# Attention stage of a hybrid encoder step: VectorE takes the low parts of step s-1 before the bias and maximum of step s+1, instead of after them

## The reference, cut to what matters

```python
def _fox_block(q, cq, qpos, k, v, ck_t, kpos):
    s = jnp.einsum('bthd,bshd->bhts', q, k) * (HEAD_DIM ** -0.5)
    bias = jnp.transpose(cq, (0, 2, 1))[..., :, None] - ck_t[:, :, None, :]
    mask = kpos[None, :] <= qpos[:, None]
    s = jnp.where(mask, s + bias, NEG_INF)
    pr = jax.nn.softmax(s, axis=-1)
    return jnp.einsum('bhts,bshd->bthd', pr.astype(v.dtype), v)
```

## Time and profile before

| | us |
|---|---|
| median of 3 runs (2385.41 to 2386.32) | 2385.94 |
| the profiled execution | 2386.21 |
| its span, first to last instruction | 2384.5 |
| TensorE busy | 2204.8 (92%) |
| VectorE busy | 1615.1 (68%) |
| ScalarE busy | 905.3 (38%) |
| GpSimd busy | 324.4 (14%) |
| attention stage, its eight heads | about 1203 to 1409 on the span's clock |

### The profile page before, as it was taken

The page is one execution under the profiler, slowest core; times in us unless marked ns, Lnnn a source line. Parts: engine busy times, 40 slices in busy tenths (PEclk is TensorE's granted clock), DMA queues, the critical chain, the costliest instruction groups (busy, mean ns, idle before and its releaser), DMA issues. The chain is left out here.

```text
span 2384.5 us, 44150 instructions
## 1 busy us (share of the span) xinstructions
PE 2204.8 (92%) x16355; PEld 2112.5 (89%) x16355; DVE 1615.1 (68%) x2941; ACT 905.3 (38%) x1843; POOL 324.4 (14%) x428
## 2 busy tenths in 40 slices
PE   3999999999899999999889978978989999999995
PEld 3999999999899999999878867978989987889995
DVE  6778766767786888876446646667657666667663
ACT  6542333333533333334366736234343331113112
POOL 0011000000111212111153410001111211111110
PEclk7999999999999999999989989989999999999997
DMA  8484444444757788786377655454556665346332
GB/s 245 145 260 111 141 131 131 149 122 143 263 187 201 225 227 230 221 231 176 112 237 226 204 176 185 131 200 148 190 207 234 217 217 164 110 123 207 103 97 98
DMA packets 362384, 424.80 MB, mean 178 GB/s; under 512 B 76064, under 2 KB 294792, under 8 KB 354336
## 3 DMA queue, kind: packets, MB, share of 16 engines
q1 hardware_dynamic: 306128, 266.62, 37.8%
q0 software_dynamic: 29504, 110.42, 13.5%
q10 hardware_dynamic: 26576, 45.40, 5.9%
HBM read 270.01 MB, written 143.68 MB: 173 GB/s over the span
## 5 line engine op out<-in xcount | busy, mean ns | idle before, releaser
L761 PE MATMUL acc<-t_act,w_hi 128*128 128x264 f32 x5376 | 888.6, 287 | 12.9 <-DVE zb L1323 5.2
L761 PEld LDWEIGHTS acc<-t_act,w_hi 128*128 128x128 f32 x5376 | 749.3, 189 | 19.5 <-issue 18.1
L761 PE MATMUL acc<-t_act,w_lo 128*128 128x264 f32 x2688 | 549.0, 286 | 0.0
L761 PEld LDWEIGHTS acc<-t_act,w_lo 128*128 128x128 f32 x2688 | 418.2, 189 | 0.0
L2764 PE MATMUL m_acc<-m_t_act,m_hi 128*128 128x264 f32 x1792 | 295.7, 288 | 19.4 <-ACT m_acc L2807 9.8
L1316 DVE TENSOR_TENSOR w_lo<-w_raw_f,w_hi 128x512 fp32r<-128x512 f32 x288 | 197.8, 687 | 143.7 <-ACT w_hi L971 143.4
L971 ACT CAST w_hi<-w_raw_f 128x512 fp32r<-128x512 f32 x288 | 177.9, 618 | 265.5 <-PE acc L761 245.0
L2764 PEld LDWEIGHTS m_acc<-m_t_act,m_hi 128*128 128x128 f32 x1792 | 252.7, 191 | 20.0 <-issue 20.0
L3171 PE MATMUL post_acc<-h_hi,w_post_hi 128*128 128x272 f32 (+1 forms) x768 | 210.9, 329 | 7.5 <-PEq L2573 4.3
L3171 PE MATMUL post_acc<-h_hi,w_post_lo 128*128 128x272 f32 (+1 forms) x768 | 208.2, 325 | 0.0
L3171 PE MATMUL post_acc<-h_lo,w_post_hi 128*128 128x272 f32 (+1 forms) x768 | 207.9, 325 | 0.0
(11 more groups left out here) (435 smaller groups left out, 3631.1 us busy)
## 6 DMA issues: line engine op xcount, KB each, us to landing
w_raw_f<-in_w_in_dram SPq DMA_DIRECT2D x96, 512.0 KB, 4.0
w_raw<-in_w_pg_dram SPq DMA_DIRECT2D x64, 512.0 KB, 4.7
cT<-zb SPq DMA_DIRECT2D x24, 1056.0 KB, 4.6
zb<-cT POOLq DMA_DIRECT2D x96, 264.0 KB, 5.8
zT<-zb POOLq DMA_DIRECT2D x80, 264.0 KB, 3.6
m_raw<-in_w_out_dram SPq DMA_DIRECT2D x32, 512.0 KB, 5.8
eT<-e_out ACTq DMA_DIRECT2D x16, 528.0 KB, 3.0
cT<-m_zb SPq DMA_DIRECT2D x8, 1056.0 KB, 5.0
```

Source lines behind the costliest of these rows:

```text
L761: mm = pe.matmul(out[:, c, 0:QN], w[:, k, :], t_act[:, SIDE[r], x, k, c * QN:(c + 1) * QN], start=(opens and k == 0 and m == 0), stop=(k = ...
```

## The change

On VectorE, in each of the eight steps of a head, the block with `low_parts` now stands ahead of the block with `bias`. Nothing is added or removed, no wait changes its condition, and the order of the other four engines is the same row for row.

```diff
             def head(h, hb, i, first=False, last=False):
                 for s in range(8):
-                    if s < 7:
-                        bias(h, s + 1, hb, i)
-                    elif not last:
-                        bias(h + 1, 0, 1 - hb, i + hb)
                     if first and s == 1:
                         for n in range(4):
                             dve.wait_ge(G["sem"][f"z_put{n}"], put_count(2 * NP - 1))
                     if s > 0:
                         low_parts(h, s - 1)
                     elif not first:
                         low_parts(h - 1, 7)
+                    if s < 7:
+                        bias(h, s + 1, hb, i)
+                    elif not last:
+                        bias(h + 1, 0, 1 - hb, i + hb)
                     if s == 1 and not first:
                         gate_out(h - 1, 1, 1 - hb)
```

## The result

The changed kernel took **2434.72 us** (median of 4 runs, 2431.32 to 2435.59), the kernel before 2386.13 us in the same comparison (4 runs, 2385.41 to 2391.34). The ratio is 1.0201, with a 95% interval of 1.0185 to 1.0218: slower by some 48.6 us. The forecast was 2429 us, in a range of 2415 to 2444. The profiled execution of the changed kernel took 2435.59 us, the slowest of the four, with a span of 2433.9 us.

What follows compares the result with a forecast made beforehand. TensorE, 95% busy, was taken to pace the attention stage. To 2386.21 us came 6.1 + 7 × 4.34 = 36.5 us for the VectorE-ScalarE ring, giving 2422.7, plus 6.5 for four clock falls: 2429 us, range 2415 to 2444.

Steps and rivals of the forecast that it cites:

- The ring: Steps 3 to 6: exponential, copy, high parts, low parts, bias, next exponential run serially; 16.00 us against 11.66, 4.34 a head.
- the first head: No earlier `weigh` covers steps 0 to 2, so all steps run serially: 21.24 us against 15.12, 6.1 us more.
- Steps 0 to 2 at nothing: Delays of about half a microsecond in steps 0 to 2 fall in idle time under the previous head's `weigh`; no cost.
- The last head: It has no copies for a next head; given the same 4.34 us as the others.
- The clock: TensorE's new pauses, about 2 us before step 7, lower its clock; four falls of 1.63 us taken, 6.5 us.
- one row each way: A 2.90 us stretch at the stage's end preceded a clock fall; a 1.60 us TensorE pause left it at 1.00.
- the prediction's rival: By the skill's rule the clock falls once or twice in every head: 2436 to 2449 us; twice has chance 0.12.
- The clock holds: Rival: TensorE's pauses stay too small to lower the clock; about 2423 us, chance 0.20.
- Two falls in every head: Rival: clock falls ahead of step 7 and in steps 4 and 5; 26.1 us extra, 2449 us, chance 0.12.
- Hidden: Rival: TensorE's work in steps 3 to 6 outlasts the serial VectorE-ScalarE chain, so nothing moves; 2386 us, chance 0.05.
- faster: Rival: earlier low parts free the transposes' banks and remove TensorE's waits, 5.3 us; 2381 us, chance 0.03.

Runs made afterwards that it cites:

- the run with the filler: Seven matmuls of 512 columns added on TensorE ahead of step 7's transposes in each head, against the changed kernel; 2425.80 us.
- the run with the copies behind: ScalarE's copies for the next head put behind the high parts in steps 3 to 6, against the changed kernel; 2418.42 us.

## Why the prediction was right, and where it was off

**What bounds the kernel.** The reading that the bias before the change runs in idle time of VectorE, and that the low parts lose nothing to it, was right. The low parts did not come earlier relative to their high parts in steps 3 to 6: in all eight heads they begin 0.03 us behind the first group, before and after, as forecast.

**The ring.** This step was right, in mechanism and size: 16.05 us against 16.00, and a head without a fall grew by 4.35 against 4.34. Steps 3 to 6 alone bring the whole loss, one step alone or every second step bring little, and taking 1.6 us of work out of the ring takes 1.6 us from a head. The estimates for the first head held too (21.32 against 21.24, 6.2 us more against 6.1). That the first period grew by 7.1 us is these 6.2, the 0.55 by which the mark moved, and the 0.34 put down to the execution. The second to the seventh head grew by 4.34 to 4.61 us between the high parts of step 2 and the low parts of step 6.

**Steps 0 to 2 at nothing.** Right for the heads with cover (25.09 against 25.05 with the change made there alone). In the first head they were in the sum. There the run with steps 0 to 2 alone gives them 1.07 us and the run with steps 3 to 6 alone gives those 5.12 (10.92 before, 16.04), which together is the 6.2 measured.

**The last head.** The prediction gave it the 4.34 us of the others, for want of a row. From the high parts of step 2 to the low parts of step 6 it took 14.44 us (1431.16 to 1445.60) where it took 9.54 (1388.03 to 1397.57): 4.90. It has no copies for a next head, so TensorE's step was shorter, and the ring in it as well.

**The clock.** This is the term that was mis-sized. The price of a fall was right where TensorE is on the path (1.63 forecast, 1.36 to 1.61 measured behind six heads, 1.6 at the stage's end), the number was not: four were taken, 6.5 us in all, and six came in the heads, 8.9 us. The forecast stood on one row each way and chose the middle. The row against a fall was also read too short: the 1.60 us of the earlier trace rows are cut out of a longer pause, which the clock came through at 1.00:

```profile
1800.35 0.72 PE L2764 MATMUL m_acc<-m_t_act,m_hi 128*128 128x264 f32 x4 [2.61 <-DVE m_zb L2944]
```

From 2429.2 to the 2435.59 of the profiled execution the steps are: falls 2.4 us, the ring of the second to the last head 1.1 (half of it in the last), the first head 0.1, the longer stretch at the stage's end 0.8, and 2.0 ahead of the low parts of the first step and behind the stage. The Trainium skill, "TensorE: Matmul & The Clock Gate", section "A second HAM failure mode: psum-queue depth-cycling", says of another kernel that short idling of TensorE between groups of matmuls, as it cycles through PSUM banks, lets the clock swing, at a price between bursts. The trace agrees that the clock swings, with a fall behind six heads. That the 2436 us of the prediction's rival, with one fall in each of eight heads, is 1.3 us above the measured median is luck: it has 13.0 us for falls, where 9.7 came, and the difference is made up by the other steps above.

**The rivals.** "The clock holds" is out, with six falls. "Two falls in every head" is out: there was one in each from the second head on. But its second place exists, as the run with the filler shows, and its price there was 0.9 us, partly hidden as the prediction's argument against it said. "Hidden" and "faster" are out by 48 us and more.

**What stays open.** Why a pause brings a fall in one head and none in the next. In the changed kernel the first head kept the clock and all later ones lost it, after the same pause of 1.74 us, and the stretches of 3.00 us ahead of `weigh(1)` read almost alike (TensorE busy 1.10 us in the first head, 1.14 in the fourth); with steps 3 to 6 alone the first head fell as well. In the run with the copies behind, three of seven nearly equal pauses (1.22 to 1.26 us) were followed by a fall. And at the stage's end TensorE pauses for 1.01 us in the kernel before and in the run with steps 0 to 2 alone, with the same instructions from there on, and only the first fell. The stretch that answers to the second of the earlier trace rows, in the run with steps 0 to 2 alone:

```profile
1399.16:1402.56 3.40, 3.40 (x16) 2.76 (x16) 1.01 (x3) 0.26 (x1) 0.00 (x0) 1.00 0.40 160
```

No run here settles what decides. That is why the count of falls could be bounded but not told.

## What to carry to other kernels

Before moving work ahead on an engine, ask whether the work it passes ran in a wait: work that fills a hole costs nothing, and the same work behind what ended the hole costs its full length. When two in-order engines hand to each other, write down one turn of the ring with every instruction that stands between, whatever it is for; the sum gave this case's ring to 0.05 us (16.00 against 16.05). And a pause that is new on TensorE can have two prices, the pause and the clock behind it. Look for the nearest pause on record for the likely number of falls, and keep none and one a turn as the bounds: here pauses of 1.74 us a head brought six and seven falls in seven heads, pauses of 1.2 us three, and pauses of 0.5 us none.

## What the runs showed of the hardware

- A pause of 1.74 us on TensorE, once in a head of 31 us, came with a fall to 0.50 for 3.4 us behind it in six of seven heads, and in seven of seven with steps 3 to 6 alone. A pause of 1.01 us at the stage's end came with one in two of six traces. A pause of 2.61 us in a later stage of the kernel before left the clock at 1.00.
- A fall of that length costs 1.4 to 1.6 us behind such a pause, and 0.9 us in steps 4 and 5, where TensorE had slack. Filling the pause with seven matmuls of 0.27 us each brought `weigh(1)` back to 0.39 us a matmul, and some falls came at another place where TensorE waits.
- The cause that the table of waits gives as issue can be a semaphore wait that is short: L2045 was issue at 0.5 us each and became a wait for low parts at 1.7 us each.
